# A two-layer decoder trunk: turns between other work of TensorE, and a last norm by token rows

## The reference, cut to what matters

```
h = rmsnorm(x);  x = x + (gated sum of HGRN2, retention, sliding-window attention) @ w_out
x = x + memory_cross_attention(rmsnorm(x), rmsnorm(mem))     # 4 heads over 256 memory tokens
x = x + peer_ffn(rmsnorm(x))                                 # 128*128 single-neuron experts
...
return rmsnorm(x, ln_final)      # x * rsqrt(mean(x*x) + 1e-6) * ln_final, after the second layer
```

## Time and profile before

| | us |
|---|---|
| median of three runs | 2484.44 |
| the profiled execution | 2484.94 |
| its span, first to last instruction | 2483.1 |
| PE busy / ACT / DVE / POOL | 2429.6 / 1322.1 / 1644.3 / 1100.0 |
| mean granted TensorE clock | 0.996 of full speed |
| DMA rate in the last ten of 40 slices, GB/s | 242, 238, 253, 205, 214, 233, 235, 236, 244, 131 |

### The profile page before, as it was taken

The page is one execution under the profiler, slowest core; times in us unless marked ns, Lnnn a source line. Parts: engine busy times, 40 slices in busy tenths (PEclk is TensorE's granted clock), DMA queues, the critical chain, the costliest instruction groups (busy, mean ns, idle before and its releaser), DMA issues.

```text
span 2483.1 us, 44363 instructions
## 1 busy us (share of the span) xinstructions
PE 2429.6 (98%) x16080; PEld 2224.3 (90%) x16080; DVE 1644.3 (66%) x3213; ACT 1322.1 (53%) x2062; POOL 1100.0 (44%) x452
## 2 busy tenths in 40 slices
PE   9999999999999999999999999999999999999998
PEld 8999988999999888888798998889999998888886
DVE  7455733787995666777774566347789955567775
ACT  5575545455555555555545655555645555554554
POOL 5865766786675000000067667767867630000000
PEclk9999999999999999999999999999999999999999
DMA  6533554455767666777654335444556676677773
GB/s 230 174 131 118 169 178 137 156 183 186 247 231 253 219 203 224 242 244 244 203 181 161 128 128 170 168 151 155 183 197 242 238 253 205 214 233 235 236 244 131
DMA packets 186555, 485.58 MB, mean 196 GB/s; under 512 B 14400, under 2 KB 80960, under 8 KB 181824
## 3 DMA queue, kind: packets, MB, share of 16 engines
q1 hardware_dynamic: 179808, 442.74, 53.9%
q10 hardware_dynamic: 6624, 41.16, 4.8%
HBM read 449.24 MB, written 34.60 MB: 195 GB/s over the span
## 4 chain that ended last, share of the span: by engine, by line
PE 89%; DVE 6%; ACT 3%; issue 1%; POOL 0%; DMA 0%; SPq 0%; DVEq 0%; ACTq 0%
PE banks L835 28%; PE banks L476 13%; PE banks L478 13%; PE banks L477 13%; PE banks L781 5%; PE banks L505 5%; PE banks L811 3%; PE banks L782 2%; PE banks L506 2%; PE banks L645 1%; DVE arena L1658 1%; ACT w_hi L867 1%; PE banks L744 1%; PE banks L728 1%; PE banks L709 1%
## 5 line engine op out<-in xcount | busy, mean ns | idle before, releaser
L406 POOL TENSOR_TENSOR w_lo<-ring,w_hi 128x1024 fp32r<-128x1024 f32 x448 | 1099.8, 2465 | 918.8 <-ACT w_hi L867 918.2
L867 ACT ACTIVATE w_hi<-ring 128x1024 fp32r<-128x1024 f32 x776 | 817.1, 1056 | 413.2 <-PE banks L835 340.2
L476 PE MATMUL banks<-h_r,w_hi 128*128 128x256 f32 x2448 | 698.3, 285 | 0.9 <-ACT arena L942 0.5
L478 PE MATMUL banks<-h_r,w_lo 128*128 128x256 f32 x2448 | 694.0, 283 | 0.0
L477 PE MATMUL banks<-h_r,w_hi 128*128 128x256 f32 x2448 | 693.9, 283 | 0.0
L835 PE MATMUL banks<-w_hi,o_r 128*128 128x512 f32 x2048 | 559.9, 390 | 0.0
L476 PEld LDWEIGHTS banks<-h_r,w_hi 128*128 128x128 f32 x2448 | 471.0, 192 | 2.7 <-issue 1.8
L477 PEld LDWEIGHTS banks<-h_r,w_hi 128*128 128x128 f32 x2448 | 471.0, 192 | 0.5 <-issue 0.5
L478 PEld LDWEIGHTS banks<-h_r,w_lo 128*128 128x128 f32 x2448 | 470.8, 192 | 0.0
L835 PEld LDWEIGHTS banks<-w_hi,o_r 128*128 128x128 f32 x2048 | 380.0, 188 | 79.2
L1865 DVE TENSOR_TENSOR w_lo<-ring,w_hi 128x1024 fp32r<-128x1024 f32 x320 | 389.6, 1218 | 31.4 <-ACT w_hi L867 31.4
(11 more groups left out here) (293 smaller groups left out, 3482.8 us busy)
## 6 DMA issues: line engine op xcount, KB each, us to landing
ring<-in_stream SPq DMA_DIRECT2D x776, 512.0 KB, 3.3
gates_dram<-o_f ACTq DMA_DIRECT2D x32, 1024.0 KB, 5.5
o_f<-gates_dram SPq DMA_DIRECT2D x32, 1024.0 KB, 7.0
arena<-in_mem ACTq DMA_DIRECT2D x2, 1024.0 KB, 13.0
arena<-in_keys ACTq DMA_DIRECT2D x2, 1024.0 KB, 6.9
arena<-in_c_decay ACTq DMA_DIRECT2D x2, 768.0 KB, 5.8
x<-in_x SPq DMA_DIRECT2D x4, 256.0 KB, 5.7
out_dram<-arena SPq DMA_DIRECT2D x4, 256.0 KB, 2.3
```

What stands on the lines that cost most here:

```text
L406: pool.tensor_tensor(w_lo[:, s, :], ring[:, s, :], w_hi[:, s, :], ALU.subtract).then_inc(sem(f"low{s}"), 1)
L476: pe.matmul(out, lhs[0], rhs[0], start=first, stop=False)
L478: return pe.matmul(out, lhs[1], rhs[0], start=False, stop=last)
L867: act.activation(w_hi[:, s, :], ring[:, s, :], ACT.Copy).then_inc(sem(f"high{s}"), 1)
```

## The change

The six edits, in the order in which they run:

1. DVE's line 1613 raises `level_ready` itself; the chain link and the separate increment go.
2. In cross-attention PE does the first value group, the turns of the probabilities, the second value group, and then the products with the values. ACT's copies of the turned probabilities lie between its two value groups. The products wait for the banks of all value tiles in two steps (before chunk 0 and before chunk 6).
3. In the selection PE and ACT alternate: turn 0, up tile, turn 1, up tile.
4. Between layers, DVE's first addition of squares goes between its work on chunks 5 and 6, and each addition raises `folded` itself.
5. In the second layer, before the down products, PE adds `x`, turned by a product with the identity, into banks 0 to 3: 16 f32 matmuls of 128 columns. The banks then end up holding `x + y` with tokens on the partitions.
6. The last norm is then done by token rows out of PSUM: ACT squares 128 x 1024 with a running sum and takes the root of one column, DVE inverts it and scales two halves of 512 by `gfin`, which is loaded as a full 128 x 1024 tile late in layer 2 by SyncE. The output is stored as token rows, in four pieces of 256 KB. The copies, turns, additions, sums by ones and the 8 scalings of before go in the second layer. The small load of `gfin` at the start goes.

```diff
-                    link(dve.tensor_tensor(halves(right, m)[:, :, 1, :], halves(qin, m)[:, :, 1, :],
-                                           halves(span, m)[:, :, 1, :], ALU.mult))
-                    dve.sem_inc(sem("level_ready"), 1)
+                    dve.tensor_tensor(halves(right, m)[:, :, 1, :], halves(qin, m)[:, :, 1, :],
+                                      halves(span, m)[:, :, 1, :], ALU.mult).then_inc(sem("level_ready"), 1)
...
-                settle()
-                with pe.Fori(0, 2) as i:
-                    token_group(G_XV + i, T_XV + i * SLOTS, mn_r)
+                token_group(G_XV, T_XV, mn_r)
                 ev("x_probs")
...
-                all_free(T_XO)
+                token_group(G_XV + 1, T_XV + SLOTS, mn_r)
                 for k in range(KC):
+                    if k in (0, 6):
+                        all_free(T_XO - 2 if k == 0 else T_XO)
...
-                with act.Fori(0, 2) as i:
-                    evac_tokens(G_XV + i, P_XV + i * 2, xv, i * SLOTS)
+                evac_tokens(G_XV, P_XV, xv)
...
+                evac_tokens(G_XV + 1, P_XV + 2, xv, SLOTS)
...
                 for t in range(NT):
+                    selection_turn(t)
                     up(G_AHEAD + PURE, t, PURE * SLOTS + t, t)
-                for t in range(NT):
-                    selection_turn(t)
...
+                if l + 1 == DEPTH:
+                    for t in range(NT):
+                        for k in range(KC):
+                            pe.matmul(bank[:, 2 * t + k // 4, k % 4 * P:(k % 4 + 1) * P], x[:, k, t * P:(t + 1) * P],
+                                      ident[:, :], start=False, stop=True, skip_group_check=True)
...
+                if l + 1 == DEPTH:
+                    for t in range(NT):
+                        if t == 0:
+                            ev("down_half", NK, NK)
+                        else:
+                            for s in range(SLOTS):
+                                used(act, l * GROUPS + GROUPS - 1, s)
+                        act.activation(square[:, 4 * t:4 * t + 4, :].rearrange("p k t -> p (k t)"), row_sum(t), ACT.Square,
+                                       accum_out=rsum[:, t:t + 1]).then_inc(sem("row_squared"), 1)
+                        act.wait_ge(sem("row_squared"), t + 1)
+                        act.activation(mx[:, t:t + 1], rsum[:, t:t + 1], ACT.Sqrt, bias=eps[:, :], scale=1.0 / D
+                                       ).then_inc(sem("row_rooted"), 1)
+                    continue
...
+                if l + 1 == DEPTH:
+                    dve.wait_ge(sem("gfin_loaded"), 16)
+                    for t in range(NT):
+                        dve.wait_ge(sem("row_rooted"), t + 1)
+                        link(dve.reciprocal(mx[:, t:t + 1], mx[:, t:t + 1]))
+                        for half in range(2):
+                            cols = slice(half * 512, half * 512 + 512)
+                            dve.scalar_tensor_tensor(y_rows[:, t, cols], bank[:, 2 * t + half, :], mx[:, t:t + 1], gfin[:, cols],
+                                                     ALU.mult, ALU.mult).then_inc(sem("final"), 1)
+                    continue
...
+                    if b == KC // 2 - 2 and l + 1 < DEPTH:
+                        fold_pair(l + 1, 1)
                 if l + 1 < DEPTH:
-                    fold_pairs(l + 1, link)
-
-            scaled(DEPTH * 3, gfin, "final")
+                    fold_pair(l + 1, 2)
```

More of the change, by code:

```diff
@@ L160, in build @@
         oml = sb("oml", [P, HEADS])
-        gfin = sb("gfin", [P, KC])
         eps_pair = sb("eps", [P, 2])
@@ L259, in build @@
         low_half = part(24832, 2, T)
+        gfin = part(25344, D)
         lbp = part(P, DEPTH, HEADS)
@@ L297, in tile_out, with row_sum @@
             return bank[:, 4 + n % 2, 0:T]
+        def row_sum(t):
+            return bank[:, 2 * t:2 * t + 2, :].rearrange("p b n -> p (b n)")
         def wide_out(n):
@@ L338, in _ @@
             load(0, 1)
-            for dst, src in ((freq[:, :], a["c_freq"]), (ident[:, :], a["c_ident"]), (iota_f[:, :], a["c_iota"]),
-                             (gfin[:, :], a["gfin"])):
+            for dst, src in ((freq[:, :], a["c_freq"]), (ident[:, :], a["c_ident"]), (iota_f[:, :], a["c_iota"])):
                 sp.dma_start(dst, src).then_inc(sem("consts"), 16)
@@ L389, in _ @@
                 refills(GROUPS - 2)
+                if l + 1 == DEPTH:
+                    sp.dma_start(gfin, a["gfin"].partition_broadcast(P).rearrange("p a d -> p (a d)")
+                                 ).then_inc(sem("gfin_loaded"), 16)
                 refills(GROUPS - 1)
@@ L392, in _ @@
                     refills(GROUPS)
[L393 to L398, removed]
+            for n in range(2 * NT):
+                sp.wait_ge(sem("final"), n + 1)
+                cols = slice(n % 2 * 512, n % 2 * 512 + 512)
+                sp.dma_start(a["out"][bass.ds(n // 2, 1), :, cols].rearrange("a p d -> (a p) d"), y_rows[:, n // 2, cols]
+                             ).then_inc(sem("stored"), 16)
+            sp.wait_ge(sem("stored"), 2 * NT * 16)
+        N_CONST = 3 * 16
         @block.gpsimd
@@ L442, in folded_pairs @@
             def folded_pairs(l):
-                for b, ready, at in ((0, "folded", l), (KC // 2 - 1, "squared", l * SQUARES + KC // 2)):
+                for b, ready, at in ((0, "folded", 2 * l), (KC // 2 - 1, "squared", l * SQUARES + KC // 2)):
                     pe.wait_ge(sem(ready), at)
@@ L848, in _ @@
                         down(G_TAIL + i, s, NK - AHEAD + i * SLOTS + s, s % 2)
[L850 to L860, removed]
+                if l + 1 < DEPTH:
+                    pe.wait_ge(sem("up_free"), l * NK + NK + 2)
+                    for t in range(NT):
+                        for k in range(KC):
+                            if k % 4 == 0:
+                                ev(f"y_out{t}{k // 4}")
+                            m = pe.transpose(bank[:, 4 + k // 2, (k % 2) * T + t * P:(k % 2) * T + (t + 1) * P],
+                                             y_rows[:, t, k * P:(k + 1) * P], ident[:, :])
+                            if t and k % 2:
+                                m.then_inc(sem("y_turned"), 1)
         @block.scalar
@@ L1211, in _ @@
                 for t in range(NT):
-                    gelu(G_AHEAD + PURE, t, t, PURE * SLOTS + t)
-                for t in range(NT):
                     ev("sel_turned", t + 1, 2)
@@ L1217, in _ @@
                                    ).then_inc(sem("sel_turned_out"), 1)
+                    gelu(G_AHEAD + PURE, t, t, PURE * SLOTS + t)
                 ev("keys_read", 6, 4)
@@ L1299, in y_out @@
                                    ).then_inc(sem(f"y_out{t}{half}"), 1)
-                if l + 1 < DEPTH:
-                    split_next(GROUPS - 1, 2)
+                if l + 1 == DEPTH:
[11 more added lines that the diff above has]
+                    continue
+                split_next(GROUPS - 1, 2)
                 ev("down_half", NK, NK)
@@ L1315, in _ @@
                 squares(KC // 2 - 1)
-            take_root(DEPTH * 3, 0)
         @block.vector
@@ L1374, in _, with fold_pair @@
             low_whole(0, 1)
[L1376 to L1382, removed]
+            def fold_pair(l, b):
+                dve.wait_ge(sem("squared"), l * SQUARES + b + 1)
+                if b > 1:
+                    dve.wait_ge(sem("folded"), 2 * l - 1)
+                o = square[:, 0:2, :]
+                dve.tensor_tensor(o, o, square[:, 2 * b:2 * b + 2, :], ALU.add).then_inc(sem("folded"), 1)
             low_whole(0, 2)
@@ L1391, in invert @@
                 dve.wait_ge(sem("inverted"), n + 1)
[L1393 to L1401, removed]
             chained = [0]
@@ L1950, in _ @@
                 tail(N_TAIL // 4 - 1, True)
[L1952 to L1955, removed]
+                if l + 1 == DEPTH:
+                    dve.wait_ge(sem("gfin_loaded"), 16)
+                    for t in range(NT):
+                        dve.wait_ge(sem("row_rooted"), t + 1)
[5 more added lines that the diff above has]
+                    continue
+                link(dve.tensor_copy(small[:, :], smalls[:, l + 1, :]))
+                for s in range(SLOTS - 1):
+                    low_whole(l * GROUPS + GROUPS, s)
                 for s in range(SLOTS):
@@ L2039 @@
         "lb": np.ascontiguousarray(by_chunk(lb_param).transpose(1, 0, 2)),
-        "gfin": by_chunk(ln_final),
+        "gfin": np.asarray(ln_final).reshape(1, D),
         "stream": stream,
@@ L2048 @@
     aps["gates"] = nc.dram_tensor("gates_dram", (CHUNKS, P, NK, CHUNK), F32, kind="Internal").ap()
-    aps["out"] = nc.dram_tensor("out_dram", (P, KC, T), F32, kind="ExternalOutput").ap()
+    aps["out"] = nc.dram_tensor("out_dram", (NT, P, D), F32, kind="ExternalOutput").ap()
     build(nc, aps)
@@ L2052 @@
     y = r.results[0]["out_dram"]
-    return np.ascontiguousarray(y.transpose(2, 1, 0)).reshape(1, T, D)
+    return y.reshape(1, T, D)
```

## The result

| us | before | after |
|---|---|---|
| median | 2484.18 (2483.84 to 2484.47) | 2458.13 (2457.6 to 2458.34) |
| span of the profiled execution | 2483.1 | 2455.8 |
| PE busy | 2429.6 | 2418.6 |
| mean granted clock | 0.996 | 0.999 |

The kernel became faster: ratio 0.9895 [0.9881, 0.9908], 26.1 us, where 21.6 us were forecast. (The medians here are of four runs each, so that of before differs a little from the 2484.44 of three on which the forecast stands.) The time lies 4.7 us under the forecast and 1.4 us under its range, so the prediction failed, on the good side. A later set of runs of the same kernel gave 0.9892.

The account below looks back on a forecast made before the run. PE, busy in 98% of the span, was taken as the bound. Terms -10.7 - 4.7 - 0.4 - 0.1 - 9.3 + 3.6 = -21.6 us took 2484.44 to 2462.8 us, range 2459.5 to 2467.5.

Parts of the forecast that it names:

- Selection: Edit 3, both layers: PE's one-hot-row wait and the half clock behind it go, 5.35 us a layer, 10.7 in all.
- Cross-attention: Edit 2, both layers: waits before the second value group and value products go, 2.34 us a layer, 4.7 in all.
- Levels: Edit 1, PE's waits at HGRN2 levels: a shorter hand-over from DVE gains 0.4 us, bounds 0 and 0.9.
- squares: Edit 4, between layers: 0.1 us gained for the chain step, bounds a 0.5 us loss and 0.7 gain.
- turn of x: Edit 5, layer 2 before the down products: 16 added f32 matmuls on PE cost 3.6 us, bounds 3.4 and 4.1.
- the estimate of 7.6 us by that rule: Edit 5: dearer alternative for the 16 plain products, four times the 1.9 us of transpose-mode turns; 3.6 was preferred.
- The end: Edit 6, last norm and store: span ends at 2473.8 instead of 2483.1, 9.3 us gained, bounds 8.3 and 9.9.
- The load at the start that goes: Edit 6, the removed small `gfin` load at the start: on no path, worth 0 to 0.3 us.
- A: Late ACT copies in selection and a new cross-attention wait: 4 us less gain, 2466.8 us; chance 0.12.
- B: Turns in new places bring half clock, 1.44 us in each of four places, 5.8 us: 2468.6; chance 0.05.
- C: Gate table's build becomes a race DVE loses; slower from 3.35 us a batch, 2489 at 3.43; chance 0.03.
- D: The end is not shortened, row norm or stores take as long: 9.3 us less, 2472.1; chance 0.04.

Follow-up runs that it names:

- layout_only: The kernel before with only the 32-byte tile `gfin` moved behind the arena, no instruction changed: 2482.48 us, ratio 0.9988 [0.9979, 0.9998].
- t56_norm: The kernel before with edits 5 and 6 alone, the small `gfin` tile gone: 2475.73 us, ratio 0.9966 [0.9954, 0.9979].
- after_padded: The changed kernel with an unused 32-byte tile in the old place of `gfin`: 2460.63 us, ratio 0.9903 [0.9886, 0.992] to the kernel before.
- arena_lower: The kernel before with the tile `esink` moved behind the arena, so the arena alone begins 32 bytes lower: one time, 2486.01 us.
- one_behind: The kernel before with PE's selection order changed to up tile, both turns, up tile: 2475.65 us, ratio 0.9962 [0.9948, 0.9976].

## Why the prediction was wrong, point by point

- **Selection: right.** Its working held step by step (ready 1.7 us early, clock up, nothing added). 11.25 us in the trace against 10.7; the rest is mainly the run-out of the turns: the end of their bar, which the next product overlaps now that it follows at once. The upper bound of 11.0 was too low for that, and for the clock: against other executions of the kernel before, the same edit takes away up to 2.8 us a layer of half clock, not 1.44.
- **Cross-attention: right, sized 0.7 low.** Both waits went whole. The missing part is again the run-out: 1.91 us is the bar, and the next product starts 379.78 - 378.11 = 1.67 us behind the first turn.
- **Levels, squares, turn of x: right** (0.5 against 0.4; 0.17 against 0.1; 3.58 against 3.6). At the squares the wait of 0.77 us is gone, and most of it comes back ahead, as foreseen. The Trainium skill (TensorE: Matmul & The Clock Gate, Terms) says that the transpose mode makes f32 four times as fast. Here 16 turns in the mode need 1.67 us from start to start and 16 plain products 3.49: a factor of 2.1, so the estimate of 7.6 us by that rule didn't come.
- **The end: right.** 9.65 against 9.3; each scaling took 0.7 us and the last store 2.5 us. No table load came between squares and root, and the large load of `gfin` on SP's queue delayed nothing that PE waited for.
- **The step that failed** is the one on edit 6's small tile: "The load at the start that goes is on no path: 0 to 0.3 us." The load is on no path indeed, but with it went the tile that lay ahead of the arena. The arena moved by 32 bytes, and PE's work in the wide output tiles, the query tiles and the spread phases became faster: 2.7 us in these two traces, 2.3 in others. The sum had no term for it, not even in its bounds. layout_only, t56_norm, after_padded and arena_lower show it in the rates; among the times, only layout_only's interval (0.5 to 5.2 us) shows it by itself.
- **Second, one execution was taken for the kernel.** The half clock's price was read from one trace. The two spans differ by further 1.24 + 0.74 us of that kind (the half clock behind the 4.16 us wait, key and query tiles at 347 or 353 ns a pair in traces of one and the same kernel), less 0.9 elsewhere, and no edit touches any of it. Here it fell in favour of the changed kernel. The forecast's reading of the list also passed over that wait: the row it calls the longest has the largest total (7.8 us), but the longest single wait is the 4.2 us of line 605.
- **The range was too narrow on this side.** With 2.7 us in the sum it would have been 2460.1, inside the range. Another 1.8 us are small terms, all low by 0.1 to 0.7, and 21.6 + 2.7 + 1.8 = 26.1 us is what the medians show. The root of the summed squares is not "about 2.5 us each way": the terms' bounds give 1.2 us towards less time and 3.2 towards more (3.9 with the 2.2 of the `gfin` load). It also took the terms' errors for independent, but most had one cause: bars were added where starts count.
- **Rivals.** A fell: neither wait came up. B fell: granted clock 1.00 behind the selection's turns and behind those of cross-attention, 3.34 us to the second batch. The Trainium skill's rule behind it (same page, Part 4: transposes don't count as busy) may hold, but turns of 0.5 to 1.7 us between products cost no clock here. C fell: the spread phase needed 180.88 us, not longer than before, with DVE's head start gone. (C's price was also added up short: 64 batches at 3.43 in place of 2.99 us are 28.2 us over the forecast, 2491 and not 2489.) D fell: the end is 9.65 us shorter.

## What to carry to other kernels

Read the price of a wait of TensorE as the wait plus the slow products after it, and that second part from several executions. Behind a wait of about 1 us the second part was nearly gone here, so a cover that leaves a short wait may bring nearly the whole gain. Where tiles are laid out one behind the other, as here, a change that removes or resizes one moves all that lie behind it; when a gain of some tenths of a per cent comes out unexplained, compare the rates of work that the change doesn't touch, and try the move of the tiles alone.

## What was not expected of the hardware

- The place of one large on-chip tile goes with the rate of rounded f32 products: with the arena where it was or 32 bytes higher, 353.4 ns for a pair of 512 and 256 columns, 32 or 64 bytes lower 346.7 ns, 16 cycles at 2.4 GHz less, in 17 of 17 traces.
- The same wait of 3.91 us is followed by a loss of 1.4 to 2.8 us to the half clock, from execution to execution; a wait of 1.04 us (one_behind) by 0.1 us at most, and 1.29 us by no slower products.
- The key and query tiles run at 347 to 348 or at 353 ns a pair in different executions of one kernel, with nothing in the program that differs.
